# Sparse-attention scores as two products of split float32 numbers, on queries stacked high over low

## The reference, cut to what matters

```python
ss = einsum('bghqd,bgqkd->bghqk', qb, ks_g) * scale     # selected keys
sw = einsum('bghqd,bgkd->bghqk', qb, kw) * scale        # window keys
out = gate0 * softmax(sc) @ vc + gate1 * softmax(ss) @ vs + gate2 * softmax(sw) @ vw
```

## Time and profile before

| | us |
|---|---|
| median of 3 runs | 1472.91 |
| lowest and highest | 1466.99, 1478.4 |
| span of the profiled execution | 1465.8 |
| PE busy | 1422.5 (97%) |
| DVE busy | 1051.1 (72%) |
| ACT busy | 871.4 (59%) |

### The profile page before, as it was taken

How to read it: one execution, slowest core, us unless ns; L and a number is a source line. 1 busy time by engine, 2 the same in 40 slices (tenths; PEclk the granted TensorE clock), 3 DMA queues, 4 the chain that set the end, 5 groups by cost and what they waited for, 6 DMA issues and landing times.

```text
span 1465.8 us, 23062 instructions
## 1 busy us (share of the span) xinstructions
PE 1422.5 (97%) x9283; PEld 1281.7 (87%) x9283; DVE 1051.1 (72%) x1601; ACT 871.4 (59%) x1522; POOL 85.3 (6%) x138
## 2 busy tenths in 40 slices
PE   8999999999999999999999989999989999999997
PEld 8988989888789989898878789998889878999886
DVE  7736669986676447699986778884776665888746
ACT  7465756564465656575545656664683553766546
POOL 9100000006000000000000000000000000000000
PEclk9999999999999999999999999999999999999999
DMA  8614476566556344665675537766545103666553
GB/s 256 189 50 151 124 228 195 180 193 190 193 145 186 80 123 144 188 189 185 188 223 199 158 116 220 214 202 191 158 145 145 45 1 104 208 191 197 185 180 115
DMA packets 189210, 240.98 MB, mean 164 GB/s; under 512 B 19086, under 2 KB 133954, under 8 KB 189104
## 3 DMA queue, kind: packets, MB, share of 16 engines
q1 hardware_dynamic: 183232, 228.66, 51.4%
q0 software_dynamic: 5776, 10.82, 2.3%
q10 hardware_dynamic: 96, 0.03, 0.0%
HBM read 238.42 MB, written 1.05 MB: 163 GB/s over the span
## 4 chain that ended last, share of the span: by engine, by line
PE 86%; ACT 5%; DVE 5%; DMA 2%; issue 1%; DVEq 0%; SPq 0%
PE bank L620 25%; PE bank L623 25%; PE bank L624 25%; PE bank L837 2%; PE bank L1222 1%; ACT w_hi L1327 1%; DVE w_lo L1883 1%; DMA raw<-in_mla_w_ukv 1%; ACT T L1824 1%; PE bank L1179 1%; PE bank L1136 1%; ACT S L1520 1%; PE bank L774 1%; PE bank L1208 1%; PE bank L900 0%
## 5 line engine op out<-in xcount | busy, mean ns | idle before, releaser
L1883 DVE TENSOR_TENSOR w_lo<-raw,w_hi 128x1024 fp32r<-128x1024 f32 (+2 forms) x452 | 518.6, 1170 | 207.9 <-ACT w_hi L1327 204.7
L1327 ACT CAST w_hi<-raw 128x1024 fp32r<-128x1024 f32 (+2 forms) x452 | 449.4, 1009 | 271.6 <-DMA raw<-in_w_in 114.3
L620 PE MATMUL bank<-h_hi,w_hi 128*128 128x256 f32 (+1 forms) x1640 | 457.4, 279 | 6.8 <-DVE h_lo L1919 3.9
L623 PE MATMUL bank<-h_lo,w_hi 128*128 128x256 f32 (+1 forms) x1640 | 454.8, 277 | 0.0
L624 PE MATMUL bank<-h_hi,w_lo 128*128 128x256 f32 (+1 forms) x1640 | 454.6, 277 | 0.0
L620 PEld LDWEIGHTS bank<-h_hi,w_hi 128*128 128x128 f32 (+1 forms) x1640 | 308.2, 188 | 10.0 <-issue 7.8
L623 PEld LDWEIGHTS bank<-h_lo,w_hi 128*128 128x128 f32 (+1 forms) x1640 | 308.2, 188 | 0.1
L624 PEld LDWEIGHTS bank<-h_hi,w_lo 128*128 128x128 f32 (+1 forms) x1640 | 308.1, 188 | 0.0
L620 PE MATMUL bank<-w_hi,h_hi 128*128 128x512 f32 (+1 forms) x464 | 178.8, 385 | 2.7 <-DVE h_lo L1919 1.7
L623 PE MATMUL bank<-w_lo,h_hi 128*128 128x512 f32 (+1 forms) x464 | 176.7, 381 | 0.0
L624 PE MATMUL bank<-w_hi,h_lo 128*128 128x512 f32 (+1 forms) x464 | 176.6, 381 | 0.0
(11 more groups left out here) (366 smaller groups left out, 2084.9 us busy)
## 6 DMA issues: line engine op xcount, KB each, us to landing
raw<-in_w_in SPq DMA_DIRECT2D x160, 512.0 KB, 3.8
raw<-in_ffn_up SPq DMA_DIRECT2D x88, 512.0 KB, 4.5
raw<-in_ffn_down SPq DMA_DIRECT2D x40, 512.0 KB, 4.4
raw<-in_w_proj_a SPq DMA_DIRECT2D x16, 512.0 KB, 3.6
raw<-in_w_proj_b SPq DMA_DIRECT2D x16, 512.0 KB, 3.5
raw<-in_w_proj_c SPq DMA_DIRECT2D x16, 512.0 KB, 3.6
raw<-in_w_out SPq DMA_DIRECT2D x16, 512.0 KB, 3.6
raw<-in_ple_gate SPq DMA_DIRECT2D x16, 512.0 KB, 4.6
```

The source lines that it names most:

```text
L620: first = pe.matmul(out_, lh, rh, start=start, stop=False)
L623: pe.matmul(out_, lh, rl, start=False, stop=False)
L1327: act.copy(weights(w_hi, slot, b, size), weights(raw, slot, b, size)).then_inc(sems["hi_done"], 1)
L1883: dve.tensor_tensor(weights(w_lo, slot, b, size), weights(raw, slot, b, size), weights(w_hi, slot, b, size).bitcast(F32), ALU.subtract).th ...
```

## The change

Queries and keys of the two big score products are now split too. `qs` holds, for each head, a tile of 128 rows: the rounded high part of its 64 rows in the half where it lies, and the low part (the remainder) in the other half. `kd_hi` and `kd_lo` hold the high and the low part of the keys, the same in both halves. The product of a stacked tile with `kd_hi` is (high + low query) x high key, and with `kd_lo` (high + low query) x low key, so two F32R products stand for one F32 product. `qs` lies in the memory of `m`, and `kd_hi` with `kd_lo` in that of `kz`. `qs` has room for two groups.

```diff
-    pe.matmul(ps[b][:, :], q2[:, 2 * g + n // 2, P:TOK],
-              kz[:, n % 2, g, :, :].rearrange("p a k -> p (a k)"), start=True, stop=False)
+    own = stacked(g, n % 2)[:, n // 2, P:TOK]
+    pe.matmul(ps[b][:, :], own, kd_hi[:, g, :, :].rearrange("p a k -> p (a k)"), start=True, stop=False)
+    pe.matmul(ps[b][:, :], own, kd_lo[:, g, :, :].rearrange("p a k -> p (a k)"), start=False, stop=False)
...
-                       q2[:, 2 * g + u, 0:P], kz[:, n, g, :, 0:P], start=False, stop=n == 1)
+        own = stacked(g, n)[:, u, 0:P]
+        for kd in (kd_hi, kd_lo):
+            mm = pe.matmul(ps[b][:, n * TOK:(n + 1) * TOK].rearrange("p (a k) -> p a k", a=2),
+                           own, kd[:, g, :, 0:P], start=False, stop=n == 1 and kd is kd_lo)
```

`scores2(g)` waits for `qs_ready` in place of `q2_ready`. ACT gets four 1024-wide copies on 64 rows ahead of the gates' read-out, and two 512-wide copies for each group:

```diff
             hi(0, 0)
             hi(0, 1)
+            act.wait_ge(sems["k2_raw"], 2)
+            for n, rows_ in enumerate((TOP, BOTTOM)):
+                for half in (TOP, BOTTOM):
+                    act.copy(kd_hi[half, n:4:2, :, :], kr2[rows_, :, :].rearrange("p (u f) n -> p f u n", u=2))\
+                        .then_inc(sems["k2_hi"], w.given("k2_hi"))
             evac("J", 0, gtT[0:48, :], ACT.Sigmoid, rows_=48)
...
+            def high_q(g):
+                act.wait_ge(sems["q2_ready"], g + 1)
+                for n, half in enumerate((TOP, BOTTOM)):
+                    act.copy(stacked(g, n, half), q2[half, 2 * g:2 * g + 2, :]).then_inc(sems["qs_hi"], w.given("qs_hi"))
+            query(0)
+            query(1)
+            high_q(0)
+            query(2)
+            high_q(1)
             preload(ACT.Exp)
             exps2(0)
+            high_q(2)
             exps2(1)
             query(3)
             turned2(0)
+            high_q(3)
```

DVE loses the two memsets and the eight copies, and gets the subtractions: four 1024-wide ones (`low_keys`) and two 512-wide ones for each group (`low_q`), each on 64 rows:

```diff
-            clear_keys()
...
-                settle(rotate2(f"keys{u}", kr2[:, 2 * u:2 * u + 2, :]))
-                for n in range(2):
-                    for par_ in range(2):
-                        ins_ = dve.tensor_copy(kz[64 * par_:64 * par_ + 64, par_, n:4:2, u, :], ...)
+                rotate2(f"keys{u}", kr2[:, 2 * u:2 * u + 2, :]).then_inc(sems["k2_raw"], w.given("k2_raw"))
...
             lo(0, 0), lo(0, 1)
+            low_keys()
             rope(0)
+            low_q(0)
             lo(1, 0), lo(1, 1)
             rope(1)
+            low_q(1)
             maxima(0)
             rope(2)
+            low_q(2)
             maxima(1)
             turned2(0)
             rope(3)
+            low_q(3)
```

More of the change, by code:

```diff
@@ L266, in program @@
         h_lo = sb("h_lo", [P, KT, TOK], F32R)
-        m = sb("m", [P, KT, TOK])
+        m = overlay([("m", [P, KT, TOK], F32)])["m"]
+        qs = sb("qs", [P, KT, TOK], F32R)
         w_hi = [sb(f"w_hi{b}", [P, PIECE + SHIFT], F32R) for b in range(RING)]
@@ L301, in program @@
              ("om", [P, 2, TT, 256], F32), ("otmp", [P, 2, 256], F32), ("Tc", [P, TT, NH, 16], F32)],
-            [kb(28), ("q2", [P, KT, TOK], F32), ("kr2", [P, 4, TOK], F32), ("kz", [P, 2, 4, 2, TOK], F32),
+            [kb(28), ("q2", [P, KT, TOK], F32), ("kr2", [P, 4, TOK], F32), ("kd_hi", [P, NG, 2, TOK], F32R), ("kd_lo", [P, NG, 2, TOK], F32R),
              ("h2_hi", [P, KT, TOK], F32R), ("h2_lo", [P, KT, TOK], F32R), ("gtT", [P, TOK], F32), ("tcT", [P, NG, TOK], F32),
@@ L323, in program @@
                "sg_ready", "u_f", "u_hi_done", "u_ready", "hn_ready", "cc_ready", "hid_ready", "gelu_ask", "gelu_done",
-               "ge_ready", "kc_ready", "vc_ready", "k2_ready", "q2_ready", "t_ready", "t_exp", "t_done", "o_hi_done",
+               "ge_ready", "kc_ready", "vc_ready", "k2_raw", "k2_hi", "k2_ready", "q2_ready", "qs_hi", "qs_ready", "t_ready", "t_exp", "t_done", "o_hi_done",
                "o_split", "final_ready", "nsa_zero", "masks_r", "h2_ready", "t_max", "tc_ready", "tc_exp", "tc_done", "o_ready", "pool_in", "pos_set", "ht_hi", "ht_ready"])}
@@ L348, in program @@
         cos2, sin2, vsw, gt, kcz, vcz = (o[k] for k in ("cos2", "sin2", "vsw", "gt", "kcz", "vcz"))
-        q2, kr2, kz, w1, cc, w2, ge, kcd, ang, posi = (o[k] for k in (
-            "q2", "kr2", "kz", "w1", "cc", "w2", "ge", "kcd", "ang", "posi"))
+        q2, kr2, kd_hi, kd_lo, w1, cc, w2, ge, kcd, ang, posi = (o[k] for k in (
+            "q2", "kr2", "kd_hi", "kd_lo", "w1", "cc", "w2", "ge", "kcd", "ang", "posi"))
         T1, T0, Tc, t1T, t0T, tcT, TcP = (o[k] for k in ("T1", "T0", "Tc", "t1T", "t0T", "tcT", "TcP"))
@@ L356, in acc, with stacked @@
             return ps[b][:, 0:n]
+        def stacked(g, n, rows_=slice(0, P)):
+            return qs[rows_, 4 * (g % 2) + n:4 * (g % 2) + n + 3:2, :]
+        TOP, BOTTOM = slice(0, 64), slice(64, P)
         def vec(l, name, t=0, n=1):
@@ L1174, in scores2 @@
             def scores2(g):
-                pe.wait_ge(sems["q2_ready"], g + 1)
+                pe.wait_ge(sems["qs_ready"], g + 1)
                 for n in range(4):
                     b = score_job(f"S{g}.{n}")
-                    pe.matmul(ps[b][:, :], q2[:, 2 * g + n // 2, P:TOK],
-                              kz[:, n % 2, g, :, :].rearrange("p a k -> p (a k)"), start=True, stop=False)
+                    own = stacked(g, n % 2)[:, n // 2, P:TOK]
+                    pe.matmul(ps[b][:, :], own, kd_hi[:, g, :, :].rearrange("p a k -> p (a k)"), start=True, stop=False)
+                    pe.matmul(ps[b][:, :], own, kd_lo[:, g, :, :].rearrange("p a k -> p (a k)"), start=False, stop=False)
                     scored(f"S{g}.{n}", pe.matmul(
@@ L1837, in high_o @@
                     .then_inc(sems["o_hi_done"], w.given("o_hi_done"))
-            for i in range(3):
-                query(i)
+            def high_q(g):
[7 more added lines that the diff above has]
+            high_q(1)
             preload(ACT.Exp)
             exps2(0)
+            high_q(2)
             exps2(1)
@@ L2496, in position_terms @@
                     dve.tensor_copy(cc[:, NG, 32 * n:32 * n + 32:2], col(ROW2[key], 16)).then_inc(sems["pos_set"], 1)
-            def clear_keys():
-                dve.memset(kz[64:P, 0, :, :, :], 0.0)
-                dve.memset(kz[0:64, 1, :, :, :], 0.0)
             ffn(0, scaled_x)
@@ L2592, in _ @@
             for u in range(2):
-                settle(rotate2(f"keys{u}", kr2[:, 2 * u:2 * u + 2, :]))
-                for n in range(2):
-                    for par_ in range(2):
-                        ins_ = dve.tensor_copy(kz[64 * par_:64 * par_ + 64, par_, n:4:2, u, :],
-                                               kr2[64 * n:64 * n + 64, 2 * u:2 * u + 2, :])
-            ins_.then_inc(sems["k2_ready"], w.given("k2_ready"))
+                rotate2(f"keys{u}", kr2[:, 2 * u:2 * u + 2, :]).then_inc(sems["k2_raw"], w.given("k2_raw"))
+                dve.wait_ge(sems["k2_raw"], w.value("k2_raw"))
             dve.wait_ge(sems["gelu_done"], w.taken("gelu_done"))
@@ L2701, in _, with low_keys, low_q @@
             tc32 = Tc[:, :, :, :].rearrange("p t h k -> p (t h) k")
+            def low_keys():
+                dve.wait_ge(sems["k2_raw"], w.value("k2_raw"))
+                for n, rows_ in enumerate((TOP, BOTTOM)):
+                    for at_, half in enumerate((TOP, BOTTOM)):
+                        dve.wait_ge(sems["k2_hi"], 2 * n + max(at_, n) + 1)
+                        ins_ = dve.tensor_tensor(kd_lo[half, n:4:2, :, :], kr2[rows_, :, :].rearrange("p (u f) n -> p f u n", u=2),
+                                                 kd_hi[rows_, n:4:2, :, :].bitcast(F32), ALU.subtract)
+                ins_.then_inc(sems["k2_ready"], w.given("k2_ready"))
+            def low_q(g):
+                for n, (half, other) in enumerate(((TOP, BOTTOM), (BOTTOM, TOP))):
+                    dve.wait_ge(sems["qs_hi"], 2 * g + n + 1)
+                    ins_ = dve.tensor_tensor(stacked(g, n, other), q2[half, 2 * g:2 * g + 2, :],
+                                             stacked(g, n, half).bitcast(F32), ALU.subtract)
+                ins_.then_inc(sems["qs_ready"], w.given("qs_ready"))
             lo(0, 0), lo(0, 1)
+            low_keys()
             rope(0)
+            low_q(0)
             lo(1, 0), lo(1, 1)
             rope(1)
+            low_q(1)
             maxima(0)
             rope(2)
+            low_q(2)
             maxima(1)
```

1 line of the change is left out of this document (removed).

## The result

The changed kernel takes 1479.5 us (median of 22 runs, 1476.8 to 1487.3), the kernel before 1475.4 us beside it (22 runs, 1467.0 to 1479.0). The ratio is 1.0035 with a 95% interval of 1.0023 to 1.0048: 5.2 us slower, 3.4 to 7.1 (the two medians alone lie 4.1 apart; I go by the ratio and its interval throughout). The forecast was +7.5 us, 1480.4, with a range of 1469 to 1487.

The account below looks back on a forecast made before the run. PE is busy 97%, but DVE and ACT were taken to pace the scores of groups 0 to 2. Waits 6.75 - 0.3 - 1.0 = +5.45, plus clock +2.0, gave +7.5 on 1472.9: 1480.4 us, range 1469 to 1487.

Parts of the forecast that it names:

- PE's saving, 10.1 us of streaming: In the 24 score jobs, F32R products save PE 0.42 us each; 10.1 us if PE set the pace everywhere.
- the first rival: ACT and DVE absorb the split work in idle time, so PE's saving arrives: 1470, or 1463 with all 10.1 us; chance 0.12.
- The key copies stop PE at the gates for 1.6 us: Four key copies on ACT, 3.87 us, delay the gates' read-out, so PE's transposes wait 1.6 us; bounds nothing to 3.9.
- The DVE list makes the first maxima 5.9 us late: Key and query subtractions on DVE, with ACT's query copies, put `maxima(0)` 5.9 us later than its old start at 1141.46.
- A new wait between the groups: DVE's `low_q(2)` waits for `high_q(2)`, queued behind `exps2(0)` on ACT; `exps2(1)` starts 7.6 us after its old start.
- `query(3)` 6.75 us late, 8.75 with the clock: After group 1's scores PE starts `query(3)` at 1159.6 instead of 1152.85, 6.75 us late; half clock adds 2.0 us.
- 0.3 and 1.0 us come back in groups 2 and 3: DVE's chain gains 0.3 us in group 2; group 3's faster scores let ACT's exponentials run unbroken, gaining 1.0 us.
- The waits alone, 5.45 forecast: Sum without the clock over the score stage: 6.75 - 0.3 - 1.0 = +5.45 us.
- The clock I took as a cost of the change alone, +2.0: After PE's new stop, groups 0 and 1 and the head of `query(3)` run at half rate about 4 us: +2.0, bounds 0 to 4.5.
- the base of 1472.9: Assumed median time of the unchanged kernel, to which the forecast +7.5 us was added.
- The rival of the half clock that stays: PE's clock stays low over groups 0 and 1 and `query(3)`, and `cs` drops again: 1483 to 1489 us; chance 0.2.
- The rule of the Trainium skill: A PE idle between bursts falls to half clock until sustained work; it made the drop after the new stop certain.

Follow-up runs that it names:

- pe_fast_only: Kernel before with each F32 score product made two F32R products, no high and low parts, no added ACT or DVE work; 1467.9 us, ratio 0.9957.
- changed_fill: Changed kernel with unused F32R filler products in all of PE's long waits; 1475.6 us, ratio 1.0006 against the kernel before.
- order_q: Changed kernel with only group 2's query split moved, behind `exps2(1)` on ACT and `maxima(1)` on DVE; 1478.9 us, ratio 1.0021 against the kernel before.
- between_fill: Changed kernel with key and query splits moved, fillers in PE's waits, and `query(3)` put ahead of `scores2(1)`; 1475.3 us, ratio 1.0003 against the kernel before.
- before_again: Kernel before, unchanged, profiled a second time; hidden layer to `values2(3)` 125.4 us against 119.4 in its first trace.
- before_fill: Kernel before with 8, 4 and 7 unused F32R products in PE's waits ahead of S2.4, X1.4 and `ct`; 1469.7 us, ratio 0.9967.

## Why the prediction was right, point by point

- *PE's saving, 10.1 us of streaming, does not come through in groups 0 to 2.* Right in kind: `scores2(0)` ran ahead and then stood 4.27 us for an exponential (5.6 forecast; the stop at the gates had already made PE late, so that less was left to wait). What the saving is worth without the added work I put at "some 3 us" in the first rival; the trace of `pe_fast_only` has 2.7, its ratio gives 6.3. The pace I took from `query(3)` for the new products was right: two score jobs of group 3 start 0.57 us apart at full clock (0.98 in the earlier trace rows):

```profile
1215.76 0.39 PE L1187 MATMUL bank<-kd_hi,qs 128*128 128x512 f32 x1
...
1216.33 0.40 PE L1187 MATMUL bank<-kd_hi,qs 128*128 128x512 f32 x1
```

- *The key copies stop PE at the gates for 1.6 us.* 1.69. Four copies took 4.26 us where I had 3.87: a single one 1.05 us on 64 rows, as on 128.
- *The DVE list makes the first maxima 5.9 us late.* 6.6: `low_keys` 4.91 instead of 4.62, and ACT's two query copies 1.26 instead of 1.09. DVE's subtraction of 64 x 512 took 0.69, the price of 128 rows. Half the rows save nothing on either engine.
- *A new wait between the groups.* There; `exps2(1)` is 9.9 us late, 7.6 forecast without the clock. `changed_fill`, with PE kept busy, has 8.4. The wait for `high_q(2)` was real but only one of two: `order_q` removed it and met `swap(2)`.
- *`query(3)` 6.75 us late, 8.75 with the clock.* `turn2(0)` right behind it: 9.05 us late, and 7.5 in `changed_fill`. So the half clock behind the stop in `scores2(0)` cost 1.5 us, where I had 2.0, and the lateness without it was 0.75 more than forecast.
- *0.3 and 1.0 us come back in groups 2 and 3.* The 0.3 didn't come. From `turn2(0)` to `ct` every trace with the splits except `between_fill` takes 27.4 us, `before_again` and `pe_fast_only` 26.8, so the change costs 0.6 us here; the 27.4 of the first trace of before contain its half clock over `cs`. The chain of the changed kernel runs through the split of the queries of group 3 at this place. From `exps2(3)` to `values2(3)` 18.4 against 18.9, and from `ct` to `exps2(3)`, where no half clock falls, 9.5 (`order_q`) against 9.9: 0.9 of the 1.0.
- *The sum.* +7.5 forecast, 5.2 (3.4 to 7.1) measured, so the forecast of the change lies just above the interval. Two terms were mis-sized. The waits alone, 5.45 forecast, are 7.3 us by the traces of the two filled kernels, 5.8 by their ratios. The clock I took as a cost of the change alone, +2.0. In fact both kernels have a half clock in this stage, and by the mean granted clocks the change adds little to it: 0.9872 over the 22 executions of the changed kernel, 0.9877 to 0.9885 over the four sets of executions of before, by the same estimate at most 1.9 us of time. That the time came out so near, 1479.5 for 1480.4, is partly luck: the base of 1472.9, from three runs, was 2.5 us low, and the change was put 2.3 us too high. The range of 1469 to 1487 would have held the unchanged time of 1475.4 as well, so it is the waits in the traces that bear the mechanism out, not the time. (The 7.1 us by which I put the profiled execution below the median compare a span with a time. Spans here are 1.8 us shorter than the time of the same execution, 1485.4 for 1487.3, so it was 5.3; nothing hangs on it.)
- *The rival of the half clock that stays* had its place in the right neighbourhood. I read the clock of before as full up to 854, but it is below full for a short time from 422 and from 538 too, and, what counts here, from 1168 to 1178. The last products of `cs` and the first scores of group 2 do run at half clock in the changed kernel (between 1184 and 1188), but so do most of `cs` and the first scores in the first trace of before, and it costs little in both. The drop that costs is the one over `values2(1)`, with and without the change.
- *The rule of the Trainium skill*, page "TensorE: Matmul & The Clock Gate", section "HAM oscillation — how this bites in real kernels". Behind the stop of 4.27 us the clock was at 0.50 in 1155 to 1157: by that rule, the trace agrees. Behind the next stop, 2.99 us, the products from 1165.42 ran at full clock, while the shorter stop at the gates, 1.69 us, was followed by 0.50 at 1134. So how long PE stood doesn't settle it in these traces. `before_fill` agrees with the rule's other half: where PE has something to do in its waits, less of the time is at half clock.

What stays open: why the ratios give the changed kernel 5.2 us over the one before where the traces give 8.2 without the half clock over `values2(1)` (134.0 - 6.4 - 119.4), and what decides whether that half clock falls. That it falls more often in the kernel before would explain the first, but the mean granted clocks don't speak for it: they are no lower in the kernel before. They count the half clock of the whole execution, though, and don't say where it falls.

## What to carry to other kernels

Ask of a product that is made cheaper by splitting its operands which engine paces the stage where it stands: here ACT's exponentials and DVE's list did, and the split was paid on exactly these. Put the split work where its engine idles, not in front of the chain's first step; in the middle of the intervals that alone moved the cost from 5.2 us to between 2.2 and 2.7, though the intervals overlap. And where a kernel is compared in steps of half a per cent, look at the granted clock behind each idle stretch of TensorE: giving it products into a free bank during its waits gained 4.9 us in the kernel before, as much as the whole change cost.

## What the runs showed of the hardware that I had not expected

Two executions of one kernel had their half clock in different places: one over most of `cs`, where it cost 0.6 us, one over `values2(1)`, where PE was busy throughout and which took 10.1 us instead of 5.3; that one cost 6.5 us, more than the change. Filler products in PE's waits, into a bank that nobody reads, raised the mean granted clock from 0.9877 to 0.9919 and gained 4.9 us. An ACT copy or DVE subtraction on 64 rows took as long as on 128 (1.05 against 1.05 us for 1024 columns on ACT, 0.69 against 0.69 for 512 on DVE).
